# Two edits of order and placement in a two-block transformer kernel: an operand half made between two key steps, and running sums in another PSUM bank

## What is computed

```python
u = rms_norm_2(h, norm_w)                       # state-space layer
z, xbc, dt = split(u @ in_w)                    # xbc: 24 chunks of 128 channels
xbc = silu(conv4(xbc) + conv_b)
dt = softplus(dt + dt_bias)
a_cum = cumsum(dt * a) within chunks of 128     # the "running sums of the step sizes"
...
h = h + out;  h = h + sigmoid(rms_norm_2(h, ple_norm_w) @ gate_w) * (p @ proj_w)
u = rms_norm_2(h, kv_norm_w);    k, v = split(u @ kv_w)       # shared keys and values
u = rms_norm_2(h, attn_norm_w);  q, gate = split(u @ attn_in_w)
```

## Time and profile before

| what | value |
|---|---|
| median of 3 runs | 958.21 us (957.85 to 958.43) |
| the profiled execution: its time | 959.5 us |
| the profiled execution: its span, first to last instruction | 957.7 us |
| PE busy | 919.1 us, 96% |
| DVE busy | 683.1 us, 71% |
| ACT busy | 524.3 us, 55% |
| mean granted clock of PE | 0.991 |

### The profile page before, as it was taken

How to read it: one execution, slowest core, us unless ns; L and a number is a source line. 1 busy time by engine, 2 the same in 40 slices (tenths; PEclk the granted TensorE clock), 3 DMA queues, 4 the chain that set the end, 5 groups by cost and what they waited for, 6 DMA issues and landing times.

```text
span 957.7 us, 14478 instructions
## 1 busy us (share of the span) xinstructions
PE 919.1 (96%) x5721; PEld 808.1 (84%) x5721; DVE 683.1 (71%) x971; ACT 524.3 (55%) x784; POOL 64.4 (7%) x67
## 2 busy tenths in 40 slices
PE   6999999999999989999999899899989998999998
PEld 6998998988888769999988699888878886778777
DVE  5688736884878678888853687875656687976655
ACT  6863332233445366666543566765756568477543
POOL 6002422430000000000000000000000000000000
PEclk9999999999999989999999899999999999999999
DMA  9543132112555455555555536543222463632232
GB/s 304 165 139 112 58 116 67 66 54 96 182 182 173 158 189 177 177 190 195 188 176 185 167 101 214 176 132 132 89 88 88 143 205 127 207 132 89 89 99 77
DMA packets 80979, 136.63 MB, mean 143 GB/s; under 512 B 3957, under 2 KB 46545, under 8 KB 80912
## 3 DMA queue, kind: packets, MB, share of 16 engines
q1 hardware_dynamic: 78800, 131.17, 41.2%
q0 software_dynamic: 2112, 4.53, 1.5%
HBM read 134.64 MB, written 1.05 MB: 142 GB/s over the span
## 4 chain that ended last, share of the span: by engine, by line
PE 63%; ACT 7%; DVE 5%; issue 4%; DMA 1%; DVEq 0%; ACTq 0%
PE bank L436 18%; PE bank L438 17%; PE bank L437 17%; PE bank L425 3%; ACT upper L1261 2%; DVE lower L1809 1%; PE bank L873 1%; PE bank L1071 1%; PE bank L1055 1%; PE bank L882 1%; ACT arena L1725 1%; PE bank L683 1%; DMA loaded<-in_ple_gate_w 1%; DMA loaded<-in_ffn_w_up 1%; ACT arena L1352 0%
## 5 line engine op out<-in xcount | busy, mean ns | idle before, releaser
L1809 DVE TENSOR_TENSOR lower<-loaded,upper 128x2048 fp32r<-128x2048 f32 x122 | 278.1, 2284 | 129.7 <-ACT upper L1261 127.7
L1261 ACT ACTIVATE upper<-loaded 128x2048 fp32r<-128x2048 f32 x122 | 231.8, 1903 | 118.0 <-PE bank L438 107.4
L436 PE MATMUL bank<-xT_upper,upper 128*128 128x256 f32 (+1 forms) x664 | 189.9, 286 | 1.1 <-DVE xT_lower L1874 1.1
L437 PE MATMUL bank<-xT_lower,upper 128*128 128x256 f32 (+1 forms) x664 | 188.2, 284 | 0.0
L438 PE MATMUL bank<-xT_upper,lower 128*128 128x256 f32 (+1 forms) x664 | 188.1, 283 | 0.0
L436 PE MATMUL bank<-upper,xT_upper 128*128 128x512 f32 (+1 forms) x360 | 146.5, 407 | 2.5 <-DVE lower L1809 1.4
L438 PE MATMUL bank<-upper,xT_lower 128*128 128x512 f32 (+1 forms) x360 | 139.4, 387 | 0.0
L437 PE MATMUL bank<-lower,xT_upper 128*128 128x512 f32 (+1 forms) x360 | 139.0, 386 | 0.0
L436 PEld LDWEIGHTS bank<-xT_upper,upper 128*128 128x128 f32 (+1 forms) x664 | 126.7, 191 | 2.4 <-issue 2.3
L437 PEld LDWEIGHTS bank<-xT_lower,upper 128*128 128x128 f32 (+1 forms) x664 | 128.2, 193 | 0.1
L438 PEld LDWEIGHTS bank<-xT_upper,lower 128*128 128x128 f32 (+1 forms) x664 | 126.7, 191 | 0.1
(11 more groups left out here) (341 smaller groups left out, 1211.8 us busy)
## 6 DMA issues: line engine op xcount, KB each, us to landing
loaded<-in_w_in SPq DMA_DIRECT2D x26, 1024.0 KB, 5.2
loaded<-in_ffn_w_up SPq DMA_DIRECT2D x22, 1024.0 KB, 5.1
loaded<-in_ssm_in_w SPq DMA_DIRECT2D x20, 1024.0 KB, 5.3
loaded<-in_ffn_w_down SPq DMA_DIRECT2D x11, 1024.0 KB, 4.9
loaded<-in_ssm_out_w SPq DMA_DIRECT2D x8, 1024.0 KB, 5.0
loaded<-in_ple_gate_w SPq DMA_DIRECT2D x8, 1024.0 KB, 5.1
loaded<-in_attn_in_w SPq DMA_DIRECT2D x8, 1024.0 KB, 5.2
loaded<-in_w_branch_ret SPq DMA_DIRECT2D x4, 1024.0 KB, 5.0
```

The source lines that it names most:

```text
L436: mm(out, a[0], b[0], start=start, stop=False)
L437: mm(out, a[0], b[1], start=False, stop=False)
L1261: A(part(upper, PARTS, n), part(loaded, LOADS, n), ACT.Copy).then_inc(uppers, 1)
L1809: TT(part(lower, LOADS, n), part(loaded, LOADS, n), part(upper, PARTS, n).bitcast(F32), sub) \
```

## The change

The running sums go to bank 4 in place of bank 6. On ACT, `norm_upper` of norm 4 for tile 0 stands before `columns_upper` of tile 1, and that for tile 1 stays. On DVE, `scale` of tile 0 stands before `row_scale(4, 1)` and `lower_rows` of tile 0 right behind it, both before `columns_lower` of tile 1; a wait for 8 of `xT2_lower_ready` stands before them. PE's order is unchanged.

```diff
@@ tensor
                 if j == 9:
                     pe.wait_ge(sem("adt_ready"), 1)
-                    ps = take(pe, ("ac",), 6)
+                    ps = take(pe, ("ac",), 4)
@@ scalar
             embed(0)
             root_table()
             other_sums(1)
+            norm_upper(4, xT, (0,))
             columns_upper(4, xT2, "kv_norm_w_2", 1)
             split_to("pg01.1", 2)
             split_to("ain0.1", -1)
-            norm_upper(4, xT)
+            norm_upper(4, xT, (1,))
@@ vector
             embed(0)
+            ve.wait_ge(sem("xT2_lower_ready"), 8)
+            scale(4, 0, xT, "attn_norm_w_2")
             row_scale(4, 1)
+            lower_rows(4, 0, xT)
             columns_lower(4, xT2, "kv_norm_w_2", 1)
             split_to("pg01.1", 2)
             ve.wait_ge(sem("xT2_lower_ready"), 16)
-            scale(4, 0, xT, "attn_norm_w_2")
-            lower_rows(4, 0, xT)
             split_to("ain0.1", -1)
             scale(4, 1, xT, "attn_norm_w_2")
             lower_rows(4, 1, xT)
```

## The result

The kernel after took 953.32 us (median of 4 runs, 952.16 to 954.67), the kernel before in the same comparison 958.32 (4 runs, 957.85 to 959.89): a ratio of 0.9945 [0.9926, 0.9965]. I had forecast 957.2, at the lowest 955.3. The profiled execution of after took 952.51 us with a span of 950.7.

The account below looks back on a forecast made before the run. TensorE, busy 96% of the span, was taken as the bound, so only its stops could pay. The terms -0.1 and -0.9 summed to -1.0 us, from a median of 958.21 to 957.2 us, range 955.3 to 958.5.

Parts of the forecast that it names:

- The wait for L2318: PE's 2.5 us wait behind the last instruction of `step_sums`; its line was to vanish from PE's waits.
- The new stops: PE would newly wait some 1.5 us in front of z0 and 0.5 to 0.9 us in front of `bR`.
- part A: Running sums into bank 4: `x_turns(3)` starts 2.65 us earlier, but later waits leave -0.1 us; ends +0.1 and -2.65.
- Kv's tile 1: Kv product of tile 1 would start 0.3 us later, as the four `scale` push `row_scale(4, 1)` back.
- DVE's stop in front of `columns_lower`: The 1.62 us stop takes in the four `lower_rows`; over 0.3 us left there would show the forecast wrong.
- part B: Tile 0's operand made between the key steps: `ain0` starts at 814.36, not 815.28; -0.9 us, ends 0 and -1.2.
- Rival 1: Hidden anyway: the 0.9 us is given back at split `ain0.1`, `ain1` weights or softmax waits; 958.1 us, chance 0.13.
- rival 2: Running-sums move pays in full: chunk 21 or the last Silu comes forward with PE; 954.6 us, chance 0.06.
- rival 5: Bank 4 isn't free at 611.6, so the stop only moves to the sums; 957.3 to 958 us, within forecast's chance.
- rival 4: Slower: a new clock drop in the kv product costs tile 1 5.7 us more; 962.9 us, chance 0.06.
- rival 3: The clock drop at 704, behind a 2.93 us stop, goes and saves 1.7 us; 955.5 us, chance 0.07.
- A median of 957.2: Whole-kernel forecast: -1.0 us from the 958.21 us median of the runs; 956.6 to 958.0 given chance 0.68.

Follow-up runs that it names:

- the four later sets: Follow-up sets, each on its own chip, running variants of before and after beside unchanged before; before's medians there: 955.55, 955.46, 955.10 and 956.88 us.
- the longer kernel: Kernel before with `step_sums` on DVE behind chunk 20 instead of 19, lengthening PE's stop to 3.94 us; 958.00 us, 1.0015 of before.

## Why the prediction was wrong, point by point

**Right in kind and size.** The wait for L2318 went. The new stops stand in front of z0 (1.60 us) and `bR` (0.56). Where the clock holds, part A is worth about what I said (0.1; 0.2 on the mean). Kv's tile 1 comes 0.37 us later (0.3 forecast), DVE's stop in front of `columns_lower` is 0.28 us, `ain0` has no stop, and part B is worth 0.85 us (0.9 forecast). It passed to the end: from `ain0` to the last matmul took 138.67 us in before and 138.55 in after. Rival 1 fell, as did rival 2 (the DVE chain didn't come forward) and rival 5.

**Wrong, first: the price of part A.** "A: -0.1" was the price of the stop in the one profiled execution, where the granted clock stayed at 1.00 behind it. In 3 of 6 profiles with this stop it didn't, and then 1.6 us more are lost. The step that failed is the one that priced the stop by its length and the waits behind it, and put a clock drop that goes with it at nothing. The term was mis-sized: on its own stretch, -0.1 should have been about -1.0 as a mean over executions, which rests on 3 drops in 6 profiles. How much of it reaches the end stays open, as 0.55 us came back behind `gate_rows`. I had weighed a drop that could come (rival 4) and one that could go at 704 (rival 3), both behind other stops; but not one that is absent from the profile shown and goes with the stop removed. Rival 4's drop exists, in the old order (4 of 10) about as often as in the new (3 of 8), so it isn't shown to be a cost of the change; it costs 1.4 to 1.6 us and not 5.7. In rival 3's place, behind `gate_rows`, the drop didn't go in after but was longer (the stretch from there to kv took 96.75 us for 95.58, and 94.4 in profiles without a drop). So that drop costs 1.1 us, for the 1.7 that rival 3 gave it, and the longer one 2.3.

**Wrong, second: the base.** "A median of 957.2" started from 958.21, the median of three runs, as if it were the kernel's level to 0.2%. This is what put the forecast off by most. The mean of before over all 144 runs is 956.23 us, between 955.7 and 957.3 in the four later sets, with executions from 952.56 to 963.76. The three runs, and the profiled execution with the slow pitch, lay in the upper part. The range of 955.3 to 958.5 held neither the two pitches (4.7 us) nor the drops (1.1 to 2.7 us each). Of the measured -5.0 us, about 2 are the change's by the later sets; about 3 aren't. In the two profiled executions nothing of the 7.0 us is the edits' but part B's 0.84: -5.0 in the up product, -1.9 ahead of it (0.65 of this the landing of the first DMA), -0.6 between the product behind up and the running sums, +0.2 in part A's stretch and +1.2 behind `gate_rows`, where after had the longer drop. That the median moved the way that was forecast is therefore in the larger part luck.

**What stays open.** What sets the pitch at a block's start isn't settled; small matmuls ahead of it may set the quick one, but the 6 profiles don't show it. Where about 3 us of the first comparison come from is open too. All four runs of before took 957.85 us or more there, as did only 31 of its other 140; if executions were independent, that would come in fewer than one case in 300. Executions close in time may share a pitch, or that comparison's chip may have differed; the runs don't tell. Above 957.7 us are 21 of the 86 executions of before in the sets that had after in them, but only 1 of the 28 of after, and the up product lies ahead of both edits. Its pitch wasn't profiled in those executions, so whether this is chance, or something in the program's layout, isn't known. And it is open how often the clock falls behind the 2.5 us stop: 3 of 6 allows for much less and much more.

## What to carry to other kernels

A stop of TensorE costs its length plus, in a share of executions, a clock drop behind it; a stop that other work "hides anyway" can therefore still be worth removing. But count the drops to the end of the kernel, since one that is avoided may turn up at the next stop. Before the gain of an edit is read from two medians of four, line up the same instructions of both traces: a difference that opens ahead of the first edit isn't the edit's. And take the spread of the unchanged kernel from many runs before a range is given, and compare a kernel only with runs of its own set.

## What the runs showed of the hardware

The steady pitch of matmuls at full granted clock has two values, 113.3 and 117.8 ns at 256 columns, 228.9 and 233.3 at 512. Some blocks had the same one in all 18 profiles, others, the up product among them, now the one and now the other.

The clock drop behind a stop isn't decided by the stop alone: 4.5 and 3.9 us always had it (18 profiles and 2), 2.9 us in 10 of 18, 2.5 us (once 2.9) in 3 of 6, 1.3 to 1.6 us in front of z0 never in 8. A drop of 3.4 us at the lower level cost 1.1 us behind `gate_rows`, 1.4 to 1.6 in the two other places; one of 6.8 us cost 2.3 behind `gate_rows` and, in the longer kernel, 2.7. On this the Trainium skill, page "TensorE: Matmul & The Clock Gate", section "HAM oscillation", tells that waits between bursts, when they are long enough, restart each burst at half the clock; the traces agree for the longest stops, and for the shorter ones only in some executions.
